# Long convolutions: filter sizes summed by channel in the input projection, filter weights scaled and summed before the filters are made, inverse transforms two chunks late

## The reference, cut to what is touched

```python
def hyena_filters(L, ...):                       # L = 512
    hdn = sin(f3 * (sin(f2 * (sin(f1 * (z @ w1 + b1)) @ w2 + b2)) @ w3 + b3))   # [L, 64]
    h = (hdn @ w4).reshape(L, 2, 2, D_MODEL)     # order, direction, channel
    h = h * exp(-t * deltas)[:, None, None, :]   # the decay
    return h / (sum(abs(h), axis=0) + EPS)       # the size, one for each filter

def bidir_long_conv(u, h_fwd, h_bwd, bias):
    k2 = concatenate([h_fwd, zeros((1, D)), h_bwd[:0:-1]], axis=0)
    return irfft(rfft(u, n=2 * L) * rfft(k2))[:L] + u * bias

u = short_conv(h @ w_in + b_in); x1, x2, v = split(u, 3)
z = v
for o, gate in enumerate((x1, x2)):
    z = gate * bidir_long_conv(z, filt[:, o, 0], filt[:, o, 1], filt_bias[o])
```

## Time and profile before

| | us |
|---|---|
| three runs | 3283.84, 3289.98, 3293.68 (median 3289.98) |
| the profiled execution | 3287.9 |
| its span | 3286.1 |
| input projection, from the first square (line 288) to the last short convolution | 670.2 to 833.4 |
| long convolutions, to the last gate | 833.4 to 1145.6 |

### The profile page before, as it was taken

The page is one execution under the profiler, slowest core; times in us unless marked ns, Lnnn a source line. Parts: engine busy times, 40 slices in busy tenths (PEclk is TensorE's granted clock), DMA queues, the critical chain, the costliest instruction groups (busy, mean ns, idle before and its releaser), DMA issues. The chain is left out here.

```text
span 3286.1 us, 32817 instructions
## 1 busy us (share of the span) xinstructions
PE 3008.9 (92%) x12672; PEld 2352.3 (72%) x12672; DVE 2076.2 (63%) x2409; ACT 1257.2 (38%) x1480; POOL 416.5 (13%) x125
## 2 busy tenths in 40 slices
PE   6897889979788789998999998999989999989998
PEld 5435766758666657777777876888868777778887
DVE  7676799778788737997456744566036566456631
ACT  4442477632111135875222233444132222344422
POOL 0201000024000010000000000344400000024442
PEclk8898899989888889999999998999989999999999
DMA  6244499722000014994322222222222222222222
GB/s 238 71 135 179 173 412 396 273 80 101 24 16 17 21 65 170 361 359 166 122 77 72 95 90 77 97 95 102 90 109 90 77 77 90 90 89 90 102 92 82
DMA packets 91293, 424.12 MB, mean 129 GB/s; under 512 B 10231, under 2 KB 15479, under 8 KB 64920
## 3 DMA queue, kind: packets, MB, share of 16 engines
q1 hardware_dynamic: 87704, 397.12, 33.5%
q10 hardware_dynamic: 3456, 25.17, 1.9%
HBM read 420.15 MB, written 2.10 MB: 128 GB/s over the span
## 5 line engine op out<-in xcount | busy, mean ns | idle before, releaser
L220 PE MATMUL psum<-h_high,weights_low 128*128 128x512 f32 x1856 | 735.7, 396 | 21.7 <-DVE h_low L339 8.6
L221 PE MATMUL psum<-h_high,weights_high 128*128 128x512 f32 x1856 | 729.9, 393 | 0.0
L222 PE MATMUL psum<-h_low,weights_high 128*128 128x512 f32 x1856 | 729.4, 393 | 0.0
L183 POOL TENSOR_TENSOR weights_low<-weights_raw,weights_high 128x2048 fp32r<-128x2048 f32 x84 | 392.2, 4669 | 2282.2 <-ACT weights_high L179 2282.2
L179 ACT ACTIVATE weights_high<-weights_raw 128x2048 fp32r<-128x2048 f32 x166 | 317.8, 1914 | 803.0 <-PE psum L222 769.4
L220 PEld LDWEIGHTS psum<-h_high,weights_low 128*128 128x128 f32 x1856 | 353.2, 190 | 107.4 <-issue 32.3
L221 PEld LDWEIGHTS psum<-h_high,weights_high 128*128 128x128 f32 x1856 | 353.3, 190 | 74.5 <-issue 1.4
L222 PEld LDWEIGHTS psum<-h_low,weights_high 128*128 128x128 f32 x1856 | 352.9, 190 | 74.6
L339 DVE TENSOR_TENSOR weights_low<-weights_raw,weights_high 128x2048 fp32r<-128x2048 f32 x82 | 187.9, 2293 | 316.7 <-ACT weights_high L179 316.7
L1579 DVE TENSOR_TENSOR weights_low<-more_raw,weights_high 128x1024 fp32r<-128x1024 f32 x168 | 203.3, 1223 | 16.6 <-ACT weights_high L1198 9.6
L2594 DVE SCALAR_TENSOR_TENSOR ff_tiles<-psum,params,ff_tiles 128x510 f32<-128x510 f32 (+1 forms) x176 | 123.7, 745 | 135.1 <-ACT ff_tiles L2572 129.1
(11 more groups left out here) (431 smaller groups left out, 4828.7 us busy)
## 6 DMA issues: line engine op xcount, KB each, us to landing
weights_raw<-in_moe SPq DMA_DIRECT2D x168, 512.0 KB, 5.6
more_raw<-in_moe SPq DMA_DIRECT2D x168, 512.0 KB, 5.6
weights_raw<-in_w_mix SPq DMA_DIRECT2D x76, 1024.0 KB, 4.9
weights_raw<-in_w_ffn SPq DMA_DIRECT2D x66, 1024.0 KB, 4.9
mod_weights<-in_ada_w ACTq DMA_DIRECT2D x24, 1024.0 KB, 8.0
mod_weights<-in_ada_w SPq DMA_DIRECT2D x32, 512.0 KB, 3.6
weights_raw<-in_hy_w_in SPq DMA_DIRECT2D x12, 1024.0 KB, 4.9
mod_weights<-in_ada_w SPq DMA_DIRECT2D x8, 1024.0 KB, 22.5
```

The lines of the kernel that those rows point to most:

```text
L183: self.nc.gpsimd.tensor_tensor(self.low[:, g % 2, :], self.raw[:, g % 2, :], self.high[:, g % 2, :].bitcast(F32), ALU.subtract).then_inc(s ...
L220: nc.tensor.matmul(out, w[1], rhs[0], start=start, stop=False)
L221: nc.tensor.matmul(out, w[0], rhs[0], start=False, stop=False)
L222: return nc.tensor.matmul(out, w[0], rhs[1], start=False, stop=stop)
```

## The change

In the input projection, the filter network's hidden layer is made in 128 rows (the 64 rows twice), so that a stack of w4's high part over its low part can be multiplied in one product. For each of 8 pieces of 128 channels (units 4 to 11) PE makes 4 tiles of raw filters by channel, two float32r products each, among the unit's own products (`size_tile`); ACT takes the absolute values; DVE multiplies by the decay laid out by channel and sums along the row (one instruction a tile) into `m.sizes`. The decay by channel is a 2 MB load, each piece of w4 a 256 KB load on SP. The rounding's low parts of the projection's weights go from POOL to DVE (`make_low_beside`). The loops over units are written out, and results go to six banks in turn.

In the long convolutions, DVE divides w4 (kept by channel) by the sizes, forms the sum and the difference of the two directions there (`weight_sums`), PE turns these (4 transposes), ACT and DVE split them into high and low, and `filters` makes the sum filter and the difference filter by 20 float32r products of 256 columns; DVE then only multiplies by the decay (`filter_decay`). Position 0 has tiles of its own (`m.first`). PSUM is now one area for z (banks 0 to 3) and one for the filter's spectrum and the inverse (banks 4 to 7). The complex multiplication of chunk i - 1 goes ahead of z's butterflies of chunk i, and the inverse of chunk i - 2 runs in chunk i.

```diff
-            ring.stream(sp, d.hy_w_in, n, following)
+            sp.dma_start(decay, d.decay_by_channel).then_inc(s.decay, 16)
...
+            for u in range(2, n + 2):
+                ring._load(sp, d.hy_w_in[u, :, :] if u < n else following[u - n, :, :])
+                if 5 <= u < 5 + pieces:
+                    piece(u - 5)
...
-            ring.make_lows(pool, n)
...
+            def size_tile(p, q):
+                x, at = 4 * p + q, slice(q * P, q * P + P)
+                if x == 0:
+                    pe.wait_ge(s.arg, 3)
+                    pe.wait_ge(s.hidden_low, 1)
+                if q == 0:
+                    pe.wait_ge(s.w4_low, p + 1)
+                if x >= 2:
+                    pe.wait_ge(s.absed, x - 1)
+                out = m.psum[:, 6 + x % 2, :]
+                nc.tensor.matmul(out, stack[:, p % 2, at], m.hidden_high[:, :], start=True, stop=False)
+                nc.tensor.matmul(out, stack[0:FILTER_WIDTH, p % 2, at], m.hidden_low[0:FILTER_WIDTH, :],
+                                 start=False, stop=True).then_inc(s.tiles, 1)
+            for u in range(n):
+                if u >= 3:
+                    pe.wait_ge(s.read_out, u - 2)
+                w = [x.rearrange("p (k m) -> p k m", k=KC) for x in ring.parts(pe, u)]
+                for i in range(2 * KC):
+                    j, k = (i % 2, i // 2) if u == 0 else (i // KC, i % KC)
+                    if u == 0 and j == 0:
+                        h_ready(k)
+                    mm = split_matmul(nc, m.psum[:, banks(u)[j], :], [x[:, k, j * P:(j + 1) * P] for x in w],
+                                      [x[:, k, :] for x in m.Hs], k == 0, k == KC - 1)
+                    if u >= lag and i % 4 == 1:
+                        size_tile(u - lag, i // 4)
+                mm.then_inc(ring.used, 1)
...
+            for u in range(n):
+                if u >= lag:
+                    for x in range(4 * (u - lag), 4 * (u - lag) + 4):
+                        act.wait_ge(s.tiles, x + 1)
+                        if x >= 4:
+                            act.wait_ge(s.normed, x - 3)
+                        nc.scalar.activation(sizes[:, x % 4, :], m.psum[:, 6 + x % 2, :], ACT.Abs).then_inc(s.absed, 1)
...
+            ring.make_low_beside(dve)
...
+                    if j and u < n - 1:
+                        ring.make_low_beside(dve)
...
+                    for x in range(4 * p, 4 * p + 4):
+                        dve.wait_ge(s.absed, x + 1)
+                        size = sizes[:, x % 4, :]
+                        nc.vector.tensor_tensor_reduce(out=size, in0=size, in1=decay[:, p, :], scale=1.0, scalar=0.0,
+                                                       op0=ALU.mult, op1=ALU.add, accum_out=m.sizes[:, x:x + 1])\
+                            .then_inc(s.normed, 1)
...
+            for i in range(2, chunks):
+                part = i % per_order
+                sp.wait_ge(s.filtered, 2 * (i - 1))
+                sp.dma_start(decays[i % 2][:, :, :], d.decay[:, :, part * N:part * N + N]).then_inc(decay_here[i % 2], 16)
...
+            def flip_z(i):
                 if i >= per_order:
-                    pe.wait_ge(s.gated, i - per_order + 1)
+                    pe.wait_ge(s.gated, 2 * (i - per_order + 1))
+                if i:
+                    pe.wait_ge(s.u_done, 2 * i)
...
+            def filters(i, sign, out):
+                w, rest = (stacks[i % 2][:, x * N:x * N + N] for x in (sign, 1 - sign))
+                for j in range(TT):
+                    at = slice(j * P, j * P + P)
+                    if j == 0:
+                        terms = [(m.first[:, 0, :], m.first[0:FILTER_WIDTH, 2, :], w),
+                                 (m.first[:, 1, :], m.first[0:FILTER_WIDTH, 3, :], rest)]
+                    else:
+                        terms = [(m.hidden_high[:, at], m.hidden_low[0:FILTER_WIDTH, at], w)]
+                    for x, (high, low, weights) in enumerate(terms):
+                        nc.tensor.matmul(out[:, j, :], high, weights, start=(x == 0), stop=False)
+                        mm = nc.tensor.matmul(out[:, j, :], low, weights[0:FILTER_WIDTH, :], start=False,
+                                              stop=(x == len(terms) - 1))
+                mm.then_inc(s.raw, 1)
...
+            flip_z(0)
+            z_spectrum(0)
+            flip_weights(0)
+            pe.wait_ge(s.w_low, 1)
+            filters(0, 0, K[:, 0:4, :])
+            filters(0, 1, K[:, 4:8, :])
+            for i in range(chunks):
+                if i:
                     z_spectrum(i)
-                if i:
-                    inverse(i - 1)
-                if i < chunks:
-                    filter_spectrum(i)
+                    pe.wait_ge(s.k_done, 2 * i)
+                else:
+                    pe.wait_ge(s.filtered, 2)
+                if i + 1 < chunks:
+                    flip_weights(i + 1)
+                if i >= 2:
+                    inverse(i - 2, 4)
+                if i + 1 < chunks:
+                    flip_z(i + 1)
+                    pe.wait_ge(s.w_low, i + 2)
+                    filters(i + 1, 0, Z[:, 4:8, :])
+                if i >= 2:
+                    pe.wait_ge(s.gated, 2 * (i - 1))
+                transform(K, 0, As[i % 2][:, 0, :, :], s.k_sums)
+                if i + 1 < chunks:
+                    pe.wait_ge(s.z_out, i + 2)
+                    filters(i + 1, 1, Z[:, 0:4, :])
+                transform(K, 1, As[i % 2][:, 1, :, :], s.k_sums)
+            pe.wait_ge(s.k_done, 2 * chunks)
+            inverse(chunks - 2, 4)
+            inverse(chunks - 1, 0)
...
+                if i:
+                    act.wait_ge(s.k_done, 2 * i)
+                for which in range(2):
+                    odds(i, s.u_sums, Z, s.u_odd, which)
+                if i == 0:
+                    weights_high(0)
+                if i + 1 < chunks:
+                    weights_high(i + 1)
+                    z_tokens(i + 1)
+                act.wait_ge(s.u_done, 2 * i + 2)
+                for which in range(2):
+                    odds(i, s.k_sums, K, s.k_odd, which)
...
+                w = w4t[:, order, tiles, :, :]
+                link(tt(w, w, sizes[:, tiles, order, :].unsqueeze(3).broadcast_to([P, 2, 2, FILTER_WIDTH]), ALU.mult))
+                fore, back = (w[:, :, x, :].unsqueeze(2).broadcast_to([P, 2, 2, FILTER_WIDTH]) for x in range(2))
+                tt(wsums[:, 0, :, :, :], fore, back, ALU.add)
+                tt(wsums[:, 1, :, :, :], fore, back, ALU.subtract).then_inc(s.w_sums, 1)
...
+            def filter_decay(i, sign, of):
+                if sign == 0:
+                    dve.wait_ge(decay_here[i % 2], 16 * (i // 2 + 1))
+                if i >= 2:
+                    dve.wait_ge(s.pairs, 2 * (i - 1))
+                dve.wait_ge(s.raw, 2 * i + sign + 1)
+                tt(As[i % 2][:, sign, :, :], of, decays[i % 2][:, :, :], ALU.mult).then_inc(s.filtered, 1)
...
-                link(nc.vector.reciprocal(rns[b], rns[b]))
-                for x in range(2):
-                    link(tt(F[:, x, :, :], F[:, x, :, :], rns[b][:, x, :].unsqueeze(1).broadcast_to([P, TT, N]), ALU.mult))
...
+            link(nc.vector.tensor_scalar(m.sizes[:, :], m.sizes[:, :], EPS, None, ALU.add))
+            link(nc.vector.reciprocal(m.sizes[:, :], m.sizes[:, :]))
+            weight_sums(0)
+            weight_sums(1)
+            for which in range(2):
+                butterflies(0, Z, F, which, s.u_odd, s.u_done)
+            weights_low(0)
+            for sign in range(2):
+                filter_decay(0, sign, K[:, 4 * sign:4 * sign + 4, :])
+            for i in range(chunks):
                 if i:
-                    multiply_imaginary(i - 1, 1)
+                    for which in range(2):
+                        butterflies(i - 1, K, Ks[(i - 1) % 2], which, s.k_odd, s.k_done)
+                    multiply(i - 1)
+                    for which in range(2):
+                        butterflies(i, Z, F, which, s.u_odd, s.u_done)
+                if i + 1 < chunks:
+                    weights_low(i + 1)
+                if i >= 2:
+                    gate(i - 2, 4)
+                if i:
                     spectrum_pairs(i - 1)
-                if i < chunks:
-                    normalise(i)
-                if i:
-                    gate(i - 1)
-                if i < chunks:
-                    for w in range(2):
-                        dve.wait_ge(s.k_odd, 2 * i + w + 1)
-                        butterflies(i, Ks[i % 2], w, s.k_done)
+                if i + 2 < chunks:
+                    weight_sums(i + 2)
+                if i + 1 < chunks:
+                    filter_decay(i + 1, 0, Z[:, 4:8, :])
+                    filter_decay(i + 1, 1, Z[:, 0:4, :])
+            last = chunks - 1
+            for which in range(2):
+                butterflies(last, K, Ks[last % 2], which, s.k_odd, s.k_done)
+            multiply(last)
+            spectrum_pairs(last)
```

(71 more changed lines are left out.)

319 lines of the change are left out of this document (146 added, 173 removed).

## The result

| | before | after |
|---|---|---|
| median, lowest to highest (us) | 3289.98, 3283.84 to 3296.09 | 3271.38, 3267.18 to 3275.13 |
| ratio, 95% interval | | 0.9942, 0.9927 to 0.9957 |
| profiled execution, span (us) | 3287.9, 3286.1 | 3267.18, 3265.4 |
| input projection, start of the first product to start of the last (us) | 686.1 to 826.9: 140.7 | 685.5 to 854.7: 169.2 |
| long convolutions, from the end of the last short convolution to that of the last gate (us) | 833.4 to 1145.6: 312.2 | 861.2 to 1126.8: 265.6 |

The kernel is faster by 0.6%, 18.6 us. The forecast was 66 us. Both phases moved as forecast in sign, and both are some way off in size: the input projection grew by 28.4 us where 13.5 were forecast, the long convolutions shrank by 46.6 where 77.7 were.

The account below looks back on a forecast made before the run. PE was taken to bound the input projection; in the long convolutions PE and DVE wait for each other. 3287.9 profiled - 77.7 (long convolutions) + 13.5 (projection) = 3223.7, said as 3224 us; range 3208 to 3252.

Parts of the forecast that it names:

- Part 1: Long convolutions, a steady chunk after the change: PE's work sums to 25.7 us, with 20 filter products at 0.135 us each.
- the upper bound: Filter products in the long convolutions: at most 0.2325 us each, today's float32 record of the same width.
- no wait above 1 us: Long convolutions, chunks 2 to 6: PE has no wait above 1 us, a sign that the forecast is right.
- The gate's cover: Long convolutions: DVE's second gate ends at 16.4 us, PE wants it at 17.2; 0.8 us, the thinnest cover.
- Part 2: Whole long convolutions phase, front to tail: 234.5 us against 312.2 today, giving back 77.7.
- Part 3: Input projection: 64 more PE products cost 14.5 us, unit 3 starts 1 us earlier; net +13.5 us.
- POOL's subtraction: Input projection: the convolution's first instruction takes 4.78 us while POOL's subtraction runs, 0.55 us alone.
- A: Long convolutions: two-chunk lag does not cover, late gate or short wait brings low clock; six chunks at 3 us, 3242; chance 0.17.
- B: Input projection: DVE bounds it, needing 15.0 us a unit against 12.7 if the convolution stays slow; 3242 us; chance 0.05.
- C: Long convolutions: new filters not cheap, float32r products of 256 columns at 0.2325 us; +15.6, 3239 us; chance 0.08.
- D: Long convolutions: TensorE stays at its lower clock level because waits cut each chunk; +206 - 64, 3430 us; chance 0.03.

Follow-up runs that it names:

- equal rows: Kernel after the change, with the second product of each pair on all 128 rows in filters and size pairs; 3215.35 us, ratio 0.9779.
- the run with the projection's edit alone: Kernel after the change, with all 128 rows in both products of the input projection's size pairs only, filters unchanged; 3260.31 us, ratio 0.9914.
- the kernels with 8, 4 or no changes a chunk: Kernel after the change, filter products reordered (8, 3247.35 us); 64 rows in both products (4, 3240.05 us); 128 rows in both (none, 3215.35 us).

## Why the prediction was wrong

The sum of the profiled execution was 3223.7, and it took 3267.2: 43.5 more. By the prediction's parts that is 14.9 in the projection, 31.1 in the long convolutions, and 2.5 less in the rest.

**Part 1, the step that failed: the price of the filters' products.** It took 0.135 us from the line through products of 384 and 512 columns, and 0.2325 as the upper bound. Measured: 0.313 at full clock and 0.51 at low clock. The price of the product by itself is 0.119 (equal rows), inside the bounds and near the lower one. What failed is the form of the neighbours. All rows that gave a price were of products behind others with the same number of rows. The upper bound was itself of 64 rows, but 16 of them stand in one run there, with two changes in all. The new kernel alternates 128 and 64 rows in each pair, and the sum had no term for that. The trace of before has rows of such a change, in the weight loads of a stretch like that of the upper bound, one chunk later:

```profile
904.80 3.32 PEld L1803 LDWEIGHTS psum<-k_spectrum,filter_hidden 64*128 64x128 f32 x16 [0.33 <-issue]
908.45 0.86 PEld L1811 LDWEIGHTS psum<-consts,x_x_v 128*128 128x128 f32 x8 [0.33 <-DVE filters_then_u L1899]
```

The first load of 64 rows behind 128, and the first of 128 behind 64, both come after 0.33 us without a load and start together with their own products (at 904.80 and 908.45); the 16 of 64 rows show no such gap between them. The Trainium skill says it too, on the page "TensorEngine Tiling (Array Packing)", section "Tiling Modes": changing the tiling mode, not just the tile, drains TensorE. The runs agree that such a change costs, and put a price on it, 0.19 us. That page was not weighed in the prediction; by its rule a sum could have had its own term for 160 changes in the long convolutions and 64 in the projection.

160 changes at 0.194 are 31.0 us. The kernel with equal rows has a phase of 226.1 us (849.8 to 1075.9) against 265.6, so the edit takes 39.5. The 8.5 beyond the 31.0 are mostly low clock: 5.0 in the three chunks of 30.0 us, and some 5 in the front and chunk 1, where a change costs more at the low level; the tail gives back 1.7. Here are two rows of the filters of chunk 0 after the change, 0.51 us apart, and then two of the kernel with equal rows, 0.21 apart: 0.30 us a change.

```profile
880.60 0.58 PE L1922 MATMUL psum<-weights_high,filter_hidden_high 128*128 128x256 f32 x1
881.11 0.58 PE L1923 MATMUL psum<-weights_high,filter_hidden_low 64*128 64x256 f32 x1
```

```profile
868.19 0.41 PE L1922 MATMUL psum<-weights_high,filter_hidden_high 128*128 128x256 f32 x1
868.41 0.41 PE L1923 MATMUL psum<-weights_high,filter_hidden_low 128*128 128x256 f32 x1
```

**Part 1, the rest of a steady chunk** was right, and its sum of 25.7 us was too high by 1.3 for the edit that it meant: 24.41. I had added lengths of records (7.14, 7.07), but what counts is from start to start: z's spectrum 908.20 to 915.11 is 6.91, and the inverse is 6.91 too. The upper bound of 0.2325 was such a length as well; from start to start it is (871.50 - 867.85)/16 = 0.228. That no wait above 1 us is left in chunks 2 to 6 was right. The gate's cover is smaller than said, 0.3 us in place of 0.8 (the gate ends at 924.19 with equal rows, PE's transform starts at 924.51), and it held.

**Part 2.** With equal rows, front 33.8 (38 forecast), chunk 1 24.6 (24), chunks 2 to 6 122.3 (128.5), chunk 7 and tail 45.5 (44): 226.1 for 234.5. As it stood: 45.1, 30.2, 146.5, 43.8, which are 265.6. The walk through the steps was sound, and all that went wrong sits where filters are made; chunk 7 and the tail, where none are, came out at 43.8 for 44. The waits of 4.4 and 4.6 us in front were in the walk.

**Part 3.** 64 products at 0.2265 us were to cost 14.5. Their 64 changes cost 12 to 13 more: a unit is 14.53 us with them and 13.04 or 12.93 without, 0.19 to 0.20 a change. The rest, 2 to 3 us, is mostly that a product of this phase now starts about 0.2325 us after the one before, not 0.2265: 82.2/354 in the window above against 82.2/363 in the earlier trace rows. The kernel after the change and the one with equal rows both show it, in units without a size pair too (11.2 us for 48 products); with one product a size tile it is 12.04/52 = 0.2315, and in the run with the projection's edit alone 12.93/56 = 0.231. Why stays open. Two windows of before show both distances at the same granted clock, so the sizes are not needed for it. The counts take in the product that a window cuts: from start to start it is 39 distances in 9.09 us in the first, 0.233, and 41 in 9.30 us in the second, 0.227. The DMA share does not sort them either: 0.33 here at 0.227, 0.31 in the kernel with equal rows at 0.2325:

```profile
2805.00:2814.00 9.00, 9.00 (x40) 1.00 0.47 167
2817.00:2826.00 9.00, 9.00 (x42) 1.00 0.33 117
```

Even without their changes the size products cost 14.9 us (64 at 0.2325), so the trace was the one to go by. The 131 ns that the Trainium skill's page "TensorE: Matmul & The Clock Gate", section "Back-to-back issue gap", has for such a product agrees with none of these rows.

That POOL's subtraction is what made the convolution's first instruction take 4.78 us was right: without POOL it takes 0.53 to 0.55 in every unit, and DVE did not become the bound.

**The rivals.** A (the lag does not cover) did not happen; the 18 us that it would cost came from elsewhere. Taking the lag away shows that it was right to count on it (6.5 us a chunk). B did not happen. C had the right place, "filters that do not become cheap", and the wrong cause, so its price (15.6 us) was less than half of the 39.5 measured. It looked at what one product costs and not at what stands next to it. D did not happen: the granted clock is 0.91 over the phase. The range ended at 3252, because its upper end added A and C, each with a ceiling from rows of the same kind; no case in it had two of PE's forms side by side.

## What to carry to other kernels

Price a new matrix product by rows with the same neighbours, and not only of the same size: read the weight loads (PEld) beside the products, and where a load starts with its own product, find out what stands before it. Products of 64 rows among products of 128 were dearer here than full ones (0.313 against 0.119 us); fewer rows than 64 were not tried. Fill the rows up (with terms that are wanted, or with zeros), or put all of one kind together. In this kernel that was worth three times what the change itself brought.

## What the runs showed of the hardware

- A change between products of 128 and of 64 rows costs 0.19 us on PE at full clock, about the same at the two widths measured (0.194 at 256 columns, 0.19 to 0.20 at 512), and 0.30 at the low level. At 256 columns the cost is linear in the number of changes (0, 4, 8, 20 a chunk). With float32 products in the attention, two changes cost 0.28.
- A float32r product of 256 columns with its weights costs 0.119 us in a row of equal ones, 0.21 at the low clock level.
- Low clock came without any wait: in every second steady chunk of the kernel after the change, the half spectrum behind the first ten of its changes ran at a granted clock of 0.68, and the half behind the other ten did not (960.00 to 966.44 us: 1.00). In the kernels with 8, 4 or no changes a chunk, steady chunks had a granted clock of 1.00. How the two are tied is not shown beyond that.
- Float32r products of 512 columns stand 0.2265 us apart or 0.231 to 0.233, for whole stretches at the same granted clock. What decides is open.
